# Attention with six score banks, one transpose bank and one gate sum per query tile, and rotation joined with key stacking, in a two-layer hybrid mixer

## The reference

```python
def softmax_probs(q, k, scale):
    s = jnp.einsum('bqhd,bkhd->bhqk', q, k).astype(jnp.float32) * scale
    return jax.nn.softmax(s, axis=-1)
# latent attention: 4 heads, 96-wide q and k, p @ v
# differential attention: 4 heads with two 32-wide maps each
p = softmax_probs(q1b, k1, scale) - lam * softmax_probs(q2b, k2, scale)
return jnp.einsum('bhqk,bkhd->bqhd', p.astype(v.dtype), v)
```

## Time and profile before

| | us |
|---|---|
| median of 3 runs (4615.93 to 4622.12) | 4619.94 |
| the profiled execution | 4612.59 |
| its span, first to last instruction | 4610.7 |
| TensorE busy in it | 3656.5 (79%) |
| VectorE, ScalarE, GpSimd busy | 2015.9, 1228.7, 1000.9 |
| mean granted TensorE clock | 0.898 of 2.4 GHz |

### The profile page before, as it was taken

One profiled execution on the slowest core, in us unless ns is written; L12 is line 12 of the kernel. 1 busy time (PEld: TensorE's weight loads), 2 busy tenths in 40 slices (PEclk: granted clock), 3 DMA queues, 4 the chain that ended last, 5 costly groups with the idle time before them and its releaser, 6 DMA issues. The chain is left out here.

```text
span 4610.7 us, 64034 instructions
## 1 busy us (share of the span) xinstructions
PE 3656.5 (79%) x25796; PEld 2830.6 (61%) x25796; DVE 2015.9 (44%) x3493; ACT 1228.7 (27%) x2126; POOL 1000.9 (22%) x1094
## 2 busy tenths in 40 slices
PE   5987888577796999895776877987687977999477
PEld 2764666456574777684662764666466755777365
DVE  4223442256535555413553323441466264554455
ACT  2101220245322323213301202220354132232340
POOL 0001101233103343222400001101332023433150
PEclk7978998789897999998997888999899988999798
DMA  4101001411101111135634101012211112111472
GB/s 168 38 36 36 26 17 50 106 41 37 57 30 55 51 46 51 48 126 163 232 102 167 53 32 45 23 34 81 78 45 39 50 48 63 53 53 42 140 248 91
DMA packets 202042, 334.47 MB, mean 73 GB/s; under 512 B 22688, under 2 KB 96160, under 8 KB 200352
## 3 DMA queue, kind: packets, MB, share of 16 engines
q1 hardware_dynamic: 172960, 283.34, 19.6%
q10 hardware_dynamic: 28800, 47.20, 2.8%
HBM read 249.45 MB, written 81.00 MB: 72 GB/s over the span
## 5 line engine op out<-in xcount | busy, mean ns | idle before, releaser
L89 PE MATMUL ps<-hh,wh_ds 128*128 128x512 f32 (+1 forms) x1600 | 705.6, 441 | 163.6 <-ACT out_ds L182 76.2
L90 PE MATMUL ps<-hl,wh_ds 128*128 128x512 f32 (+1 forms) x1600 | 619.5, 387 | 0.0
L91 PE MATMUL ps<-hh,wl_ds 128*128 128x512 f32 (+1 forms) x1600 | 619.3, 387 | 0.0
L89 PEld LDWEIGHTS ps<-hh,wh_ds 128*128 128x128 f32 x1600 | 325.2, 203 | 253.0 <-ACT out_ds L182 86.5
L195 POOL CAST wh_ds<-raw_ds 128x512 fp32r<-128x512 f32 x160 | 104.7, 654 | 1228.7 <-DMA raw_ds<-in_d_win 400.7
L90 PEld LDWEIGHTS ps<-hl,wh_ds 128*128 128x128 f32 x1600 | 326.2, 204 | 57.7 <-issue 20.0
L91 PEld LDWEIGHTS ps<-hh,wl_ds 128*128 128x128 f32 x1600 | 322.6, 202 | 58.3
L1968 DVE TENSOR_TENSOR T_dr<-T_dr,ps 64x256 f32<-64x256 f32 x400 | 167.6, 419 | 220.1 <-PE ps L1725 210.8
L1137 ACT ACTIVATE qk_da<-ps,nmx_d 128x1280 f32<-128x1280 f32 (+1 forms) x144 | 177.8, 1235 | 300.7 <-DVE nmx_d L1065 259.3
L1866 ACT ACTIVATE TT_dr<-ps 128x512 f32<-128x512 f32 x200 | 117.3, 597 | 398.7 <-PE ps L1715 396.6
L197 POOL TENSOR_TENSOR wl_ds<-raw_ds,wh_ds 128x512 fp32r<-128x512 f32 x160 | 209.7, 1311 | 12.8
(11 more groups left out here) (328 smaller groups left out, 7970.6 us busy)
## 6 DMA issues: line engine op xcount, KB each, us to landing
gate_sums<-out_ds ACTq DMA_DIRECT2D x160, 256.0 KB, 2.0
raw_ds<-in_d_wmerge SPq DMA_DIRECT2D x128, 256.0 KB, 2.7
logit_mg<-gate_sums SPq DMA_DIRECT2D x128, 256.0 KB, 3.4
w_mod<-in_d_wmod SPq DMA_DIRECT2D x12, 2048.0 KB, 20.1
R_dr<-decay_rows SPq DMA_DIRECT2D x80, 256.0 KB, 4.3
q_raw_da<-turned_qk SPq DMA_DIRECT2D x288, 32.0 KB, 1.9
acc_ou<-merged SPq DMA_DIRECT2D x18, 512.0 KB, 5.2
raw_ds<-in_d_win SPq DMA_DIRECT2D x32, 256.0 KB, 2.7
```

The costliest lines, as they stand in the source:

```text
L89: pe.matmul(out, w_hi, x_hi, start=first, stop=False)
L90: pe.matmul(out, w_hi, x_lo, start=False, stop=False)
L91: return pe.matmul(out, w_lo, x_hi, start=False, stop=last)
```

## The change

- `attention`: the score regions are three banks each (banks 0 to 5), so that a unit's scores no longer wait for the exponential of the unit before; one maximum over 1280 takes the place of two and the joining step. All transposes go through bank 6 in groups of 4, 4 and 2, woven between the score pieces; each group waits for the copy of the one before. Gate sums move to bank 7, which the values also use: one chunk for each query tile (2 k-steps at each of four spots), none in the last tile; the first spot waits for the output of the tile before, and the values wait until ScalarE has moved the chunk (`settled`). Both value pairs are issued in head 2, the first behind the first score piece, the second at its end. Gate weights are loaded and cut once per tile.
- `prepare_maps` takes the place of `rotate_columns` and `stack_maps` for the differential branch, with 64 k-steps of gate sums in the place of 80; queries are written after turn 4, keys after turn 8, and the keys come back in four groups with gate weights between them.
- `expand_latents`: two heads per matmul, 128 rows wide, six banks.
- `normalise_rows`: the low part goes to GpSimd, with the four weight cuts between.
- `delta_rule`: two gate-sum points come earlier. `normalise_columns`, `rotate_columns`, `normalise_turned`: weight cuts two steps later.
- `apply_gates`: three slots, ScalarE's high part and VectorE's low part one piece behind. By the plans it is left 368 k-steps (46 chunks) in layer 0 and 104 (13 chunks) in layer 1.

The core of the diff, in the order of the file:

```diff
                 mm.then_inc(self.made, 1)
             self.q += 1
+    def settled(self, pe):
...
+        if self.q:
+            pe.wait_ge(self.moved, self.q // KD)
...
             @block.gpsimd
             def _(pool):
-                m.dense.cut(pool)
+                for t in range(NT):
+                    pool.wait_ge(high, t + 1)
+                    pool.tensor_tensor(m.hl[:, :, t * P:(t + 1) * P], h[:, t % 2],
+                                       m.hh[:, :, t * P:(t + 1) * P].bitcast(F32), ALU.subtract).then_inc(low, 1)
+                    if t in (1, 3, 5, 7):
+                        m.dense.cut(pool, None, m.dense.half + 1)
...
+            jobs.append((width, [(wq[:, j, 0:P], raw[:, j, cols]) for j in range(2)], [(qr[:, cols], slice(0, P))]))
+            for pair in range(HEADS // 2):
+                own = slice(2 * pair * NOPE, 2 * (pair + 1) * NOPE)
+                halves = [slice(a * NOPE, (a + 1) * NOPE) for a in range(2)]
+                jobs.append((width, [(wq[:, j, P:][:, own], raw[:, j, cols]) for j in range(2)],
+                             [(q[0:NOPE, 2 * pair + a, cols], halves[a]) for a in range(2)]))
+                jobs.append((width, [(wkv[:, own], raw[:, 2, cols])],
+                             [(k[0:NOPE, 2 * pair + a, cols], halves[a]) for a in range(2)]))
...
+    SPOTS = 4
     fill = m.dense
-    fill.plan(n_tiles * UNITS, rate, (5,))
+    fill.plan((n_tiles - 1) * SPOTS, KD // SPOTS, (7,))
...
+            def scores(h, a):
+                at = 3 * 512 * (h % 2 if maps == 1 else a)
+                return flat[:, at:at + keys]
+            def turn_bank(count):
+                return m.ps[:, 6, 0:count * P]
...
-                        fill.load(sp, g * maps)
+                    fill.load(sp, SPOTS * (i - 1))
...
-                    if g != 1 and (g == 2 or u > 0):
-                        back, g_last = (0, 0) if g == 2 else (1, G - 1)
...
-                        pe.wait_ge(moved, (u - 1) * len(movers) + (movers.index(g) + 1))
+                    last = u * G + g - 1
+                    if last >= 0:
+                        movers, moved = (on_act, moved_a) if last % G in on_act else (on_dve, moved_d)
+                        pe.wait_ge(moved, last // G * len(movers) + movers.index(last % G) + 1)
                     for b in range(count):
                         src = e[:, h % 2, maps - 1, (at + b) * P:(at + b + 1) * P]
-                        mm = pe.transpose(turn_bank(g, count)[:, b * P:(b + 1) * P], src, m.ident)
...
+                        fill.settled(pe)
...
+                def spot(i, point):
+                    if point == 1:
+                        pe.wait_ge(y_done, i + 1)
+                    fill.tensor(pe, SPOTS * i + point)
...
+                        if maps == 1:
+                            turns = {0: [0], 1: [1], 2: [2]}
+                        else:
+                            turns = {1: [0], 3: [1], 5: [2]}
                         for a in range(maps):
...
                             if n >= 2:
                                 pe.wait_ge(exp_done, n - 1)
-                            for at, width in far:
-                                mm = score(i, h, a, at, width)
-                            if far:
-                                mm.then_inc(scored_wide, 1)
-                            if a == 0 and i and h % 2 == 0:
-                                value(i - 1, h // 2)
-                            for g in range(G) if before else ():
-                                if maps == 1 or (g > 0) == (a > 0):
-                                    turn(*before, g)
-                            fill.tensor(pe, n + 1)
-                            if split and n >= 1:
-                                pe.wait_ge(exp_done, n)
-                            score(i, h, a, *near).then_inc(scored, 1)
-                i = n_tiles
+                            for x, (at, width) in enumerate(pieces):
+                                mm = pe.matmul(scores(h, a)[:, at:at + width],
+                                               qs[:, h] if maps == 1 else qs[:, (i * HEADS + h) % 3, a],
+                                               k_all(h, a)[:, at:at + width], start=True, stop=True)
+                                if x == len(pieces) - 1:
+                                    mm.then_inc(scored, 1)
+                                if h == 2 and i and a == 0 and x == 0:
+                                    value(i - 1, 0)
+                                if x == len(pieces) - 1 and a == 0:
+                                    if h == 3 and i < n_tiles - 1:
+                                        spot(i, 1)
+                                    if h == 0 and i:
+                                        spot(i - 1, 2)
+                                    if h == 1 and i:
+                                        spot(i - 1, 3 if maps == 2 else 4)
+                                if before:
+                                    for g in turns.get(x + a * len(pieces), ()) if G > 1 else ():
+                                        turn(*before, g)
+                            if before and G == 1 and a == maps - 1:
+                                turn(*before, 0)
+                            if h == 1 and i and a == 1:
+                                spot(i - 1, 4)
+                        if h == 2 and i:
+                            value(i - 1, 1)
+                i = n_tiles - 1
                 for h in range(HEADS - LAG, HEADS):
-                    value(i - 1, h - HEADS + LAG) if h % 2 == 0 else None
                     for g in range(G):
-                        turn(i - 1, h, g)
-                fill.tensor(pe)
-                value(i - 1, PAIRS - 1)
+                        turn(i, h, g)
+                    value(i, h - HEADS + LAG)
...
-                    dve.reduce_max(mx[:, h, a:a + 1], rest(r), AX.X).then_inc(dve_step, 1)
+                    dve.reduce_max(mx[:, h, a:a + 1], scores(h, a), AX.X).then_inc(dve_step, 1)
                     dve.wait_ge(dve_step, n + 1)
...
                         if before:
-                            move(*before, on_dve)
+                            move(*before, on_dve[:1])
+                        for a in range(maps):
+                            find((i * HEADS + h) * maps + a, h, a)
+                            if a == 0 and maps == 2 and (i or h):
+                                mix(*((i, h - 1) if h else (i - 1, HEADS - 1)))
+                        if before:
+                            move(*before, on_dve[1:])
                             if maps == 1:
                                 invert(before[1])
                         if maps == 1 and i and h == LAG - 1:
                             keep(i - 1)
-                        for a in range(maps):
-                            find((i * HEADS + h) * maps + a, h, a)
-                            if a == 0 and maps == 2 and (i or h):
-                                mix(*((i, h - 1) if h else (i - 1, HEADS - 1)))
-                                if i and h == LAG:
-                                    finish(i - 1)
-                i = n_tiles
+                i = n_tiles - 1
                 if maps == 2:
...
-                        if maps == 1 and i and h == LAG:
+                        if i and h == LAG:
+                            fill.move(act, SPOTS * i)
+                        if maps == 1 and i and h == LAG + 1:
...
-                fill.move(act)
+                    move(i, h, on_act)
...
+    TURNS = 8
     fill = m.dense
-    fill.plan(MAPS, 6)
...
+    fill.plan(TURNS + MAPS, 4)
+    steps = [(qk[:, j], c) for j in range(4) for c in (1, 2)]
...
+            sp.dma_start(perm, m.d_const[:, C_PERM]).then_inc(table_in, 16)
+            sp.dma_start(cos, m.d_rope).then_inc(table_in, 16)
+            sp.dma_start(vecs, m.d_bvec[l:l + 1, B_LAM:B_LAM + 4 * ROPE].to_broadcast([P, 4 * ROPE])).then_inc(vecs_in, 16)
+            fill.load(sp, 1)
+            sp.wait_ge(rotated, 4)
+            sp.dma_start(m.d_qk[:, 0:2], raw[0]).then_inc(q_out, 16)
+            fill.load(sp, 4)
+            sp.wait_ge(rotated, 8)
+            sp.dma_start(m.d_qk[:, 2:4], raw[1]).then_inc(k_out, 16)
+            sp.wait_ge(q_out, 16)
+            sp.wait_ge(k_out, 16)
+            for g in range(4):
+                if g >= 2:
+                    sp.wait_ge(k_low, 2 * (g - 1))
+                src = m.d_qk[:, 2 + g // 2].rearrange("(j r) c -> r j c", r=ROPE)[:, 2 * (g % 2):2 * (g % 2) + 2]
+                for n in range(4):
+                    sp.dma_start(raw[g % 2][ROPE * n:ROPE * n + ROPE], src).then_inc(k_in[g % 2], 16)
+                fill.load(sp, 5 + 2 * g)
             fill.load(sp)
...
                 dve.wait_ge(k_high, j + 1)
-                dve.tensor_tensor(kk[low, j], raw[j // 4][low, j % 4], kk[low, j].bitcast(F32), ALU.subtract
```

(27 more changed lines are left out.)

259 lines of the change are left out of this document (115 added, 144 removed).

## The result

The changed kernel takes 4656.40 us as the median of 4 runs (4637.01 to 4661.43), the kernel before in the same session 4617.93: a ratio of 1.0077, 95% interval 1.0045 to 1.0108. It is 0.8% slower; 4475 was forecast. The profiled execution took 4637.01 (span 4635.2), against 4612.59 before; it is the fastest of the four, 19 us under their median. I work with these two, since their phases can be laid side by side.

The account below looks back on a forecast made before the run. TensorE was taken as mostly dense, with a ring of waits pacing differential attention. Terms -52 - 48 - 8 - 38 - 27 - 47 - 14 - 8 + 100 = -142 took 4612.6 to 4471, given as 4475 us; range 4410 to 4560.

Parts of the forecast that it names:

- Part 1: Differential attention over all keys: -52 us in layer 0, -48 in layer 1, and -8 over the context keys.
- the ring: Differential attention: one head's chain of dependent steps across engines takes 5.4 us, giving a tile of 29.3 us against 34.2.
- The upper bound: Differential attention: a query tile takes at worst the 34.2 us of the kernel before.
- Rival (a): Differential attention: one transpose bank's three-copy chain keeps the tile at 34.2 us, +100, total 4572; chance 0.12 with (d).
- Rival (b): Differential attention: staging sets the pace, GpSimd's subtraction taking 1.3 us, tile 32 us, +43, total 4518; chance 0.15.
- Rival (d): Differential attention: scores still held by something else, the same as (a) in time; chance 0.12 together with (a).
- Rival (c): Differential attention: with less filler TensorE's clock falls to half, tile 40 us, total 4662, slower than before; chance 0.07.
- Part 2: Latent attention: waits for copies of transposes mostly go, -14; -20 us and, with the context tiles, -18.
- Part 5: `normalise_rows`: low part on GpSimd relieves VectorE, -7 us a layer, -14 in all, with 3 for mutual interference.
- Part 6: Small changes: `delta_rule` gate matmuls move into waits, -8 us; weight cuts two steps later 0, bounds ±4.
- Parts 3, 4 and 7: `expand_latents` -27 us; `prepare_maps` -16 and -31, `apply_gates` +53 and +47 in layers 0 and 1.
- the signs that I listed: Trace signs, right: tiles 29 us apart, GpSimd's preparation gap under 20; wrong: tiles over 33, PEclk under 0.8.

Follow-up runs that it names:

- experiment 1: Changed kernel with ScalarE's third transpose copy moved ahead of the second exponential in differential attention: 4556.5 us, ratio 0.9878 to the kernel before.
- experiment 2: Changed kernel with eight unread matmuls per head before the first transposes in differential attention: 4686.0 us, ratio 1.0152 to the kernel before.
- experiment 6: Changed kernel with no gate sums in any attention, all done in `apply_gates`: 4689.0 us, ratio 1.0149 to the kernel before.
- experiment 4: Changed kernel with the weight cut in `normalise_columns` back at its old place: 4685.3 us, ratio 1.0149 to the kernel before.

## Why the prediction was wrong

The profiled execution was forecast at 4471 and took 4637, a miss of 166 us, and the phases give it back:

| part | forecast | measured | miss |
|---|---|---|---|
| 1, differential attention, layers 0 and 1 | 300, 247 | 370.3, 314.1 | +137 |
| 2, latent attention | 242, 212.5 | 253.9, 231.0 | +30 |
| 3, `expand_latents` | 30.8, 29.1 | 29.3, 29.2 | -1 |
| 4, `prepare_maps` | 73, 76 | 76.2, 78.6 | +6 |
| 5, `normalise_rows` | 49.9, 49.8 | 60.2, 60.8 | +21 |
| 6, `delta_rule` | -8, layers together | -2.9, -2.2 | +3 |
| 6, weight cuts later | 0 | -33 in four phases | -33 |
| 7, `apply_gates` | 231, 100 | 231.8, 100.8 | +2 |

**Part 1 failed, at the ring.** "A copy out of PSUM with its signal 0.65 ..., third transpose group ..., two score pieces ..., first group" puts one copy on the path, the second group's, and goes from the third group straight to the next head's first. With a single transpose bank there is one more link between those two: the copy of the third group, and the diff queues it behind the second exponential. I had the wait (each group waits for the copy of the one before) and the copy in hand, but did not ask what stands ahead of that copy in ScalarE's queue. The ring is 7.84 us and not 5.4. Experiment 1 takes the exponential out of that link and recovers 88 of the 137. In its heads of 5.53 us the third copy (0.39) still lies between the two groups, beside the two score pieces that I had there; that these nearly cover it is luck of the layout, and the other terms were right.

**The upper bound failed too.** I took "the 34.2 of now" as the worst tile. Nothing bounded it: a new wait can make a ring longer than the old one. 37.5 was measured. Rival (a) named the place, one transpose bank and three copies per head, but by the same bound its price ended at +100, and so its case could not come out slower.

The rest of part 1, 49 us, is in experiment 1. Of the 24 in layer 1, 10 are six tiles of 31.0 us for 29.3, in which the second values at the lower clock level have up to 1.6 each; 11.5 are the start, with the first output at 62.5 us for 51; and 2 the end. The 25 in layer 0 are not broken down. At the start of layer 1 stands one head of 13.5 us. There GpSimd cuts two weight halves (3216.3 to 3225.1) before it stages the next queries, at 3228.9, where the forecast had the cuts at nothing because staging is "three slots deep"; with one half per head this stall is gone, as the version with spread cuts shows.

Rival (b), staging as the pace, did not come: GpSimd's subtraction took 0.865 us and not 1.3, and TensorE waited 20.3 us for queries, five times in the layer. Rival (d) is out with the 0.2 us that scores wait for an exponential.

**Rival (c) came near in time, 4662 for 4656, and is wrong as the cause.** The granted clock fell to 0.76 and 0.83, and the kernel became slower. But the ring takes 7.84 us with the clock at 1.00, experiment 2 raises the clock and lengthens the stage, and experiment 6 lowers it to 0.66 and 0.70 and shortens the stage. The clock rose when the wait was shortened (experiment 1) and when it was filled (experiment 2), so it fell because TensorE stood waiting. I had priced half clock at 11 us a tile; the estimate from the rows is 2.3. So of the 8.2 us by which the tile of layer 1 missed (37.5 for 29.3), the clock has about a quarter and the ring the rest. That (c)'s time came out is luck. The Trainium skill (TensorE: Matmul & The Clock Gate, A second HAM failure mode: psum-queue depth-cycling) describes such swings between the two levels where a kernel cycles through PSUM banks. The trace agrees that they are there, between 0.70 and 1.00 from one head to the next.

**Part 2** had the term "the waits for copies of transposes mostly go, -14". They fell from 18.6 to 8.4 us in layer 1. I left out two waits that the change brings in the same bank and queue: values that wait until ScalarE has moved the gate chunk, and queries whose staging stands behind both weight cuts of a tile (12.2 us, of which 7.9 were there before). The waits of TensorE in latent attention of layer 1:

```profile
PE ps L979 <- POOL qs_la L903: 12.2, 4, 7.6
PE ps L948 <- ACT out_ds L187: 8.9, 7, 1.3
PE ps L933 <- ACT work_la L1101: 4.6, 11, 0.8
PE ps L933 <- DVE work_la L1019: 3.8, 4, 1.4
```

So the waits are 31 us together, as many as before, and TensorE's busy time fell by 2.5 us where one chunk less was to give 5.6; the stage took 231.0 for 232.5. The version with the cuts spread over the heads, which here also writes the outputs later, gave 7.4 us back, though the wait for queries only fell from 12.2 to 8.8; the rest of that gain, and the wait on the gate chunk, were not tried apart.

**Part 5** had the wrong sign. I allowed 3 us for GpSimd and VectorE in each other's way; it was 10.5 in one line. And I had the last part end 1.8 us behind VectorE; with two parts left it was 3.8 (55.6 to 59.4). The Trainium skill (SBUF — State Buffer, Who interferes with whom) was cited for VectorE instructions with two SBUF inputs. The same section names a second kind, copies, casts and `tensor_scalar` in a mode with two ports, and says that of such an instruction and one of GpSimd the first to issue blocks the other for its whole length. The trace agrees: L341 is a `tensor_scalar` with one tensor, source and result in SBUF, and it is the step that went from 0.81 to 2.12 us, while the statistics and the scaling beside it kept their durations (12.7 and 13.6 us in all).

**Part 6** cost the later cuts at nothing, with bounds of 4. They gave 33 us (experiment 4): the cut stood ahead of the squares that TensorE waits for. I had looked at when the halves are needed and not at what is queued behind them, the same fault as in part 1, with the other sign.

**Parts 3, 4 and 7 held**, within 1, 6 and 2 us; these were sums of counted instructions and transfers on one engine that is the bound. Of the signs that I listed, the scores' wait for the exponential and the 68 rows of `expand_latents` came out as said, and GpSimd's gap in the preparation at 22.8 us for "under 20"; ScalarE's idle time of 106.5 before the exponential, the tile over 33 and a PEclk under 0.8 were signs of wrong.

## What to carry to other kernels

When several operations share one bank or buffer, follow every reuse of it through the queue of the engine that frees it, and write down what is queued ahead of the freeing instruction; here one copy placed behind an exponential cost 92 us, and a weight cut placed ahead of a product 33. A cut or load queued ahead of staged data can also close a circle of waits. A tile's present period is no upper bound for a new ring. A clock that falls together with a stage's busy share is first a sign of waiting, here with a quarter of the tile's miss as its own share: read the ring where the clock is full, and add and remove filler, before it is called the cause.

## What was not expected of the hardware

- VectorE's normalising step over 128x1024 float32 took 0.81 us without and 2.12 us beside GpSimd subtractions of the same size, which took 2.341 each; the eight steps that met one cost 10.5 us of the 12.3 that the move was to bring.
- Half the granted clock cost a head of the ring, with no gate sums in it, about 0.6 us: 8.39 at 0.50, 7.84 at 1.00. A lower granted clock and a shorter stage went together: with PEclk at 0.70 in place of 0.83 differential attention was 13.4 us shorter, for the gate sums were off the ring's value stretch.
- A gate chunk costs 5.6 us where TensorE is the bound, and 3.4 inside the ring of differential attention in layer 1, where TensorE is idle for 84 of 271 us.
